# Order of weight splits and new rows, place of the output rows and explicit table loads in a decoder kernel on one core

## Chip, cores and metric

One Trainium2 chip, one of its cores. The metric is the device time of one launch in microseconds: the median over runs. The engines are TensorE (PE in the profile, its weight loads PEld), VectorE (DVE), ScalarE (ACT), GpSimd (POOL) and SyncE (SP), which here only issues DMAs.

## What is computed

The input is x of 256 rows by 1024 columns, fp32. It passes through two blocks of layers, ten residual steps in all:

```python
f = swiglu(rmsnorm(h, g0)) @ w_down;  h = h + 0.5 * rmsnorm(f, g1)     # ffn, four times
h = h + rmsnorm(retention(rmsnorm(h, g2)), g3)                          # layer 0
h = h + rmsnorm(stick_breaking(rmsnorm(h, g2)), g3)                     # layer 1
gate = sigmoid(rmsnorm(h, g6) @ ple_gate); h = h + rmsnorm(gate * (p @ ple_proj), g7)   # twice
h = h + short_conv(rms_norm(h, n0))                                     # second block
h = h + moba(rms_norm(h, n1))                                           # last attention
```

The last attention (moba) has 16 heads of width 64. With 256 rows there is one block of keys, so each head is a causal softmax of q k' with a slope on the distance; q and k are normed per head, and the output rows are multiplied with silu(z) before the last matrix. Everything is fp32 to within small errors, so each matrix product is done as three: high part by high part, high by low, low by high.

## The kernel before

**Weights.** All matrices are streamed once. A slot is 256 rows by 512 columns (512 KB). SP loads it into one of 4 raw buffers (`load_slot`, line 342), each load waiting until DVE has made the low part of the slot four before. ACT rounds it to w_hi (`split`, line 976), DVE makes w_lo = raw - w_hi (`split`, line 1388). w_hi and w_lo are rings of 8 slots; TensorE waits for w_lo (`products`, line 490). `split_to(n)` on either engine means: do all splits up to slot n here. Since the engines run their lists strictly in order, the places of these calls are the schedule, and they are written out by hand.

**Products.** For one slot and one half t of the rows (128 rows) TensorE does six products of 128x128 by 128x512 (lines 497 to 499, two chunks c of three). An "in" phase (`in_proj`, and `ffn` for the four swiglu phases) goes in groups: group m is row half t = m % 2 of 512 output columns, four slots deep (one slot in ple_proj). Groups 2k and 2k + 1 use the same four slots. An "out" phase (`out_proj`) has four groups, two halves by 1024 columns; its last `window` slots (8 for ple_gate, so all of them; 4 where the phase has 8 slots; else 6) are done first for t = 0 and then for t = 1. The order of phases is that of `phase_list` (line 116): ffn_in0, down0, ret_in, ret_out, ffn_in1, down1, ple_proj0, ple_gate0, ffn_in2, down2, sb_in, sb_out, ffn_in3, down3, ple_proj1, ple_gate1, conv_in, conv_out, moba_in, moba_out.

**Boundaries.** After each out phase come new rows h. Boundary b = 0 is the start, 1 down0, 2 ret_out, 3 down1, 4 ple_gate0, 5 down2, 6 sb_out, 7 down3, 8 ple_gate1, 9 conv_out. For each half t and each half q of the columns: TensorE transposes h (`turn_h`, line 531, four transposes), DVE multiplies with the gain into xg (line 1406), ACT rounds to x_hi (line 992), DVE makes x_lo (line 1411). TensorE's group t waits for x_lo of its first half q = 0 before slot 0 and of q = 1 before slot 2 (line 520). Half t = 0 is turned two slots before the end of the out phase. Half t = 1 is turned within group 0 of the next phase: q = 0 after its slot 1, q = 1 after its slot 2 (`turn_new`, line 527), except for boundaries 3 and 7, where `ple` turns it between the groups of ple_proj.

DVE's x_part (line 1401) makes both xg first and then both x_lo:

```python
for q in range(2):
    ... xg[q] = turn[2t + q] * gain          # waits for the transposes
for q in range(2):
    ... x_lo[q] = xg[q] - x_hi[q]            # waits for ACT's x_hi[q]
```

In an out phase DVE and ACT do, in this order: reading of t = 0, splits, x_part(b, 0), reading of t = 1 (ACT: squares of the sums, line 1011, or in ple_gate the sigmoid, line 1165; DVE: gain and residual sum, lines 1422 and 1430), then in the next phase x_part(b, 1). POOL makes the root of the squares between ACT and DVE. In ACT's `start` (line 1038) there are splits up to slot 6 of the phase before x_part(b, 1), then squares of h, then splits up to slot 8. In ACT's `ple` (line 1145) x_part(b, 1) and the squares stand before the fourth copy of sums and the splits of ple_proj's slots 6 and 7, which are slots 4 and 5 of the gate.

**Start.** DVE: gains, x_part(0, 0), splits 0 to 3, then x_part(0, 1). ACT: split 0, x_part(0, 0), split 1, squares, splits up to 5, x_part(0, 1).

**The last attention.** In moba_in groups 8 to 15 TensorE, DVE and ACT run stages 0 to 7 of a pipeline over pairs of heads behind each group (`mb_stage` in three versions). Stage k: TensorE scores of pair k, output of pair k - 2, transposes of the softmax weights of pair k - 1 (`mb_turn_p`, line 855). ACT: copies of the weights of pair k - 1 (line 1330), negated maxima (line 1335) and exponentials (line 1339) of pair k, then two splits. DVE: rows of pair k - 2, distance term and maxima of pair k (lines 1832 to 1837). Groups 12 to 15 are z, which ACT reads with Silu (line 1036). Silu and Exp need different tables; the compiler puts a load before the first activation that needs another table, behind the waits that stand before it.

The first output rows (heads 0 to 3) are turned by `mb_turn_y(0, 0)` (line 895) on TensorE after group 15, ahead of stage 7. ACT makes y_hi of them (line 1344) before it copies the sums of group 15, behind stage 6 and its two splits; DVE makes y_lo (line 1613) behind the same splits. `mb_turn_p(13)`, in stage 7, waits for that y_lo, since it writes the same PSUM bank. Stage 8 runs behind slot 0 of moba_out, stage 9 behind slot 1. In stage 8 `mb_turn_p(15)` waits for y_lo of the next four heads (`mb_turn_y(0, 1)`), which ACT makes behind stage 7; `mb_turn_y(0, 1)` itself waits for ACT's copies of the weights of heads 12 and 13.

Of the kernel before, what the change touches and what calls it, by code (L numbers as in the profile page):

```python
# [36 lines left out]
SC = 2  # L37
# [3 lines left out]
BANKS = 4  # L41
# [171 lines left out]
def build(nc, x, p_in, positions, norm_gains, ffn_w_gate, ffn_w_up, ffn_w_down, ret_w_in, ret_gn_gain,  # L213
          ret_w_out, sb_w_in, sb_w_out, ple_w_gate, ple_w_proj, norm_g_2, conv_w_in_2, conv_w_2,
          conv_w_out_2, attn_w_in_2, q_norm_g_2, k_norm_g_2, attn_w_out_2, consts, out):
    with ExitStack() as ctx:
# [272 lines left out]
        def _(pe):  # L489
            def products(bank, t, n, j, c0, hi, lo, first, last, sign):  # L490

                pe.wait_ge(lo_made, lin(n + 1, RING, j))
                rows = slice(t * P, (t + 1) * P)
                for c in range(SC):
                    a, b = hi[:, c0 + c, rows], lo[:, c0 + c, rows]
                    wh, wl = w_hi[:, n % RING, c, :], w_lo[:, n % RING, c, :]
                    pe.matmul(bank[:, :], a, wh, start=(first and c == 0), stop=False, skip_group_check=True)  # L497
                    pe.matmul(bank[:, :], a, wl, start=False, stop=False, skip_group_check=True)  # L498
                    mm = pe.matmul(bank[:, :], b, wh, start=False, stop=(last and c == SC - 1), skip_group_check=True)  # L499
                if sign is not None:  # L500
                    mm.then_inc(sign, 1)
# [10 lines left out]
            def group(ph, m, hi, lo, j=None, hooks={}, new_x=None):  # L512
# [4 lines left out]
                for s in range(per):  # L517
# [5 lines left out]
                    products(sums[(ph.group0 + m) % BANKS], t, n, j, SC * s, hi, lo, s == 0, last, sign)  # L523
# [3 lines left out]
            def turn_new(b):  # L527

                return {1: lambda: turn_h(b, 1, [0]), 2: lambda: turn_h(b, 1, [1])}
# [356 lines left out]
            def mb_turn_y(half, i):  # L886
# [6 lines left out]
                for c in range(2):  # L893
                    for t in range(NT):
# [7 lines left out]
                     15: lambda: (mb_turn_y(0, 0), mb_stage(7))}  # L902
            hooks.update({8 + k: lambda k=k: mb_stage(k) for k in range(7)})
            in_proj("moba_in", 9, hooks, {10: {2: lambda: mb_turn(1, 1)}})
# [61 lines left out]
        def _(act):  # L966
# [71 lines left out]
            def start(ph, b):  # L1038

                split_to(ph.slot0 + 6)  # L1040
                x_part(b, 1)
                h_squares(b, 1)
                split_to(ph.slot0 + 8)
# [279 lines left out]
            def mb_stage(k):  # L1323

                for hd in range(2 * k - 2, 2 * k) if 1 <= k < MH // 2 + 1 else ():
# [4 lines left out]
                    act.activation(work[:, at + 384:at + 768], mb_p_bank(hd)[:, 0:384], ACT.Copy).then_inc(mb["pt_flat"], 1)  # L1330
                for hd in range(2 * k, 2 * k + 2) if k < MH // 2 else ():
# [15 lines left out]
            for m in range(16):  # L1347
# [11 lines left out]
                if m == 15:  # L1359
                    mb_y_hi(0, 0)  # L1360
# [24 lines left out]
        def _(dve):  # L1385
# [15 lines left out]
            def x_part(b, t):  # L1401
# [7 lines left out]
                for q in range(2):  # L1409
# [134 lines left out]
            x_part(0, 0)  # L1544
# [306 lines left out]
            for k in range(8):  # L1851
                if k == 7:
                    mb_y_lo(0, 0)
                mb_stage(k)
# [37 lines left out]
```

## Time and profile before

| | us |
|---|---|
| median of 3 runs | 1411.66 |
| lowest, highest | 1410.5, 1412.23 |
| the profiled execution | 1412.48 |
| its span in the trace | 1410.7 |
| PE busy | 1389.1 (98%) |
| DVE busy | 845.5 (60%) |
| ACT busy | 728.6 (52%) |
| POOL busy | 66.3 (5%) |
| mean DMA rate | 178 GB/s |

A row of the timeline is: start in us, duration in us, engine, line of the kernel, operation, output <- input, shape, how many are merged, and in brackets the idle time before it and what ended it. The next instruction of ACT or DVE starts about 0.1 us before the end of the one before, so a queue of them is shorter than the sum of durations. Products of 128x512 follow each other every 0.2275 us at full clock though each lasts 0.39: they are pipelined. The granted clock of TensorE is 1.00 at 2.4 GHz and 0.50 at 1.2 GHz.

### The profile page before, as it was taken

Reading aid. Unit: us, or ns where it says so; the run is one execution under the profiler, and the core shown is the slowest. Engines: PE = TensorE matmul, PEld = TensorE weight load, DVE = VectorE, ACT = ScalarE, POOL = GpSimd, SP = SyncE. Lnnn points to the kernel's source line nnn. Section 1 sums busy time; section 2 is a strip of 40 time slices with the busy share of each in tenths; the row PEclk is TensorE's granted clock in tenths of the full one; section 3 lists DMA queues with packets and bytes.
Section 4 is the critical chain, followed back from the end, with each engine's and each line's share of the span. In section 5 each row is a group of like instructions: output and inputs, shape, how many; then the busy total and the mean of one; then the engine's idle time right before and its main releaser. Section 6 shows DMA issues by size and latency. Waiting matters only on the chain. (4 is left out here: it accounts for less than half of the span.)

```text
span 1410.7 us, 19001 instructions
## 1 busy us (share of the span) xinstructions
PE 1389.1 (98%) x6458; PEld 1143.5 (81%) x6458; DVE 845.5 (60%) x1066; ACT 728.6 (52%) x1026; POOL 66.3 (5%) x117
## 2 busy tenths in 40 slices
PE   8999999999999999999999999999999999999998
PEld 6888888888888888878888888878888878888776
DVE  6555766666665555575555554575555675577665
ACT  5444454444454445474444455664444565555683
POOL 1000010000010000010000000010000110002000
PEclk9999999999999999999999999999999999999998
DMA  7656545555645666446567554455666455545431
GB/s 241 190 185 207 183 158 190 180 190 192 201 139 188 194 207 219 153 148 212 178 197 236 164 179 135 135 164 178 188 214 231 143 180 193 182 152 174 147 120 61
DMA packets 186525, 251.41 MB, mean 178 GB/s; under 512 B 15540, under 2 KB 115420, under 8 KB 186460
## 3 DMA queue, kind: packets, MB, share of 16 engines
q1 hardware_dynamic: 186172, 250.43, 55.0%
q8 instruction: 39, 0.64, 0.2%
q14 instruction: 26, 0.21, 0.0%
q10 hardware_dynamic: 288, 0.13, 0.0%
HBM read 249.45 MB, written 1.05 MB: 178 GB/s over the span
## 5 line engine op out<-in xcount | busy, mean ns | idle before, releaser
L1392 DVE TENSOR_TENSOR w_lo<-raw,w_hi 128x1024 fp32r<-128x1024 f32 x460 | 539.6, 1220 | 181.8 <-ACT w_hi L980 180.7
L980 ACT ACTIVATE w_hi<-raw 128x1024 fp32r<-128x1024 f32 x460 | 460.6, 1051 | 135.4 <-PE sums L499 66.9
L497 PE MATMUL sums<-w_hi,x_hi 128*128 128x512 f32 x1312 | 522.4, 398 | 4.8 <-DVE x_lo L1411 3.7
L499 PE MATMUL sums<-w_hi,x_lo 128*128 128x512 f32 x1312 | 512.4, 391 | 0.0
L498 PE MATMUL sums<-w_lo,x_hi 128*128 128x512 f32 x1312 | 511.5, 390 | 0.0
L497 PEld LDWEIGHTS sums<-w_hi,x_hi 128*128 128x128 f32 x1312 | 246.9, 188 | 58.3 <-issue 9.9
L499 PEld LDWEIGHTS sums<-w_hi,x_lo 128*128 128x128 f32 x1312 | 246.5, 188 | 52.1
L498 PEld LDWEIGHTS sums<-w_lo,x_hi 128*128 128x128 f32 x1312 | 247.2, 188 | 49.2 <-issue 1.0
L497 PE MATMUL sums<-w_hi,y_hi 128*128 128x512 f32 x512 | 202.0, 395 | 0.0
L498 PE MATMUL sums<-w_lo,y_hi 128*128 128x512 f32 x512 | 200.0, 391 | 0.0
L499 PE MATMUL sums<-w_hi,y_lo 128*128 128x512 f32 x512 | 200.0, 391 | 0.0
L1053 ACT ACTIVATE work<-sums,stat 128x256 f32<-128x256 f32 x88 | 41.7, 474 | 239.9 <-PE sums L499 239.9
L1468 DVE SCALAR_TENSOR_TENSOR work<-sums,stat,work 128x256 f32<-128x256 f32 x88 | 42.4, 482 | 180.4 <-ACT work L1053 180.4
L499 PEld LDWEIGHTS sums<-w_hi,y_lo 128*128 128x128 f32 x512 | 96.5, 189 | 20.3
L497 PEld LDWEIGHTS sums<-w_hi,y_hi 128*128 128x128 f32 x512 | 96.7, 189 | 19.7
L498 PEld LDWEIGHTS sums<-w_lo,y_hi 128*128 128x128 f32 x512 | 96.6, 189 | 19.5
L1036 ACT ACTIVATE work<-sums,stat 128x512 f32<-128x512 f32 x54 | 37.1, 687 | 129.8 <-PE sums L499 128.6
L992 ACT ACTIVATE x_hi<-xg 128x512 fp32r<-128x512 f32 x40 | 24.8, 630 | 47.3 <-DVE xg L1406 47.0
L924 POOL TENSOR_TENSOR stat<-stat,neg_half 128x1 f32<-128x1 f32 (+1 forms) x48 | 46.3, 964 | 4.0
L938 POOL TENSOR_TENSOR stat<-stat 128x1 f32<-128x1 f32 x16 | 3.6, 223 | 906.6 <-ACT junk L1011 865.1
L1422 DVE TENSOR_TENSOR fg<-sums,post_gain 128x512 f32<-128x512 f32 x24 | 16.6, 692 | 33.3 <-ACT junk L1011 33.1
L1011 ACT ACTIVATE junk<-sums 128x512 bf16<-128x512 f32 x24 | 14.2, 593 | 37.3 <-PE sums L499 37.2
(171 smaller groups left out, 780.9 us busy)
## 6 DMA issues: line engine op xcount, KB each, us to landing
raw<-in_ffn_w_gate_dram SPq DMA_DIRECT2D x176, 256.0 KB, 3.9
raw<-in_ffn_w_up_dram SPq DMA_DIRECT2D x176, 256.0 KB, 4.8
raw<-in_ffn_w_down_dram SPq DMA_DIRECT2D x176, 256.0 KB, 3.9
raw<-in_ret_w_in_dram SPq DMA_DIRECT2D x96, 256.0 KB, 4.0
raw<-in_conv_w_in_dram SPq DMA_DIRECT2D x64, 256.0 KB, 4.0
raw<-in_attn_w_in_dram SPq DMA_DIRECT2D x64, 256.0 KB, 3.9
raw<-in_sb_w_in_dram SPq DMA_DIRECT2D x48, 256.0 KB, 3.6
raw<-in_ret_w_out_dram SPq DMA_DIRECT2D x32, 256.0 KB, 4.5
```

Of the source, the lines that this page charges most:

```text
L497: pe.matmul(bank[:, :], a, wh, start=(first and c == 0), stop=False, skip_group_check=True)
L498: pe.matmul(bank[:, :], a, wl, start=False, stop=False, skip_group_check=True)
L499: mm = pe.matmul(bank[:, :], b, wh, start=False, stop=(last and c == SC - 1), skip_group_check=True)
L924: pool.tensor_tensor(dst, tmp, neg_half[:, 0:k], ALU.pow).then_inc(sign, 1)
L980: act.activation(w_hi[:, n % RING].rearrange("p c n -> p (c n)"), raw[:, n % RAW].rearrange("p c n -> p (c n)"), ACT.Copy).then_inc(hi_mad ...
L992: act.activation(x_hi[:, 4 * q:4 * q + 4, t * P:(t + 1) * P], xg[:, q, :].rearrange("p (c t) -> p c t", c=4), ACT.Copy).then_inc(x_hi_made, 1)
L1011: act.activation(junk[:, 0:COLS], sums[(ph.group0 + 2 * t + n) % BANKS][:, :], ACT.Square, accum_out=f_sq[:, 2 * t + n:2 * t + n + 1]).the ...
L1036: act.activation(dst, sums[(ph.group0 + m) % BANKS][:, :], func, **kw).then_inc(act_read, 1)
L1053: act.activation(work[:, t * FB:(t + 1) * FB], sums[(ph.group0 + m) % BANKS][:, 0:FB], ACT.Silu, scale=r_in[:, t:t + 1]).then_inc(act_read, 1)
L1392: dve.tensor_tensor(w_lo[:, n % RING].rearrange("p c n -> p (c n)"), raw[:, n % RAW].rearrange("p c n -> p (c n)"), w_hi[:, n % RING].rear ...
L1422: dve.tensor_tensor(fg[:, t, n, :], sums[(ph.group0 + 2 * t + n) % BANKS][:, :], post_gain[:, n * COLS:(n + 1) * COLS], ALU.mult).then_inc ...
L1468: dve.scalar_tensor_tensor(out=work[:, HW_HID + t * FB:HW_HID + (t + 1) * FB], in0=sums[(ph.group0 + m) % BANKS][:, FB:2 * FB], scalar=r_i ...
```

## The change

1. Boundaries: DVE's x_part makes xg and x_lo of q = 0 and then xg and x_lo of q = 1. TensorE turns the second half of the rows later: q = 0 in the middle of slot 2 of group 0 instead of after slot 1, q = 1 after slot 2 as before; behind a ple phase (b = 4 and 8) q = 0 after slot 2 and q = 1 in the middle of slot 3. `products` gets a hook after its first chunk for that.
2. Start: DVE makes the low part of slot 0 between xg and x_lo of q = 0. ACT makes splits up to 3, not 5, before x_part(0, 1).
3. Last attention: mb_turn_y(0, 0) stands in the middle of the last slot of group 15; ACT's y_hi of it stands in stage 6 between the copies of weights and the exponentials, DVE's y_lo behind stage 6, ahead of its two splits.
4. ACT loads the table of the exponentials by an explicit instruction in stages 0 and 4 to 7, behind the copies of weights and before the wait for the maxima.

```diff
@@ products (line 490)
-            def products(bank, t, n, j, c0, hi, lo, first, last, sign):
+            def products(bank, t, n, j, c0, hi, lo, first, last, sign, between=None):
...
                     mm = pe.matmul(bank[:, :], b, wh, start=False, stop=(last and c == SC - 1), skip_group_check=True)
+                    if between and c == 0:
+                        between()
@@ group (line 512)
-                    products(sums[(ph.group0 + m) % BANKS], t, n, j, SC * s, hi, lo, s == 0, last, sign)
+                    products(sums[(ph.group0 + m) % BANKS], t, n, j, SC * s, hi, lo, s == 0, last, sign, hooks.get((s, 0)))
                     if s in hooks:
                         hooks[s]()
@@ turn_new (line 527)
-                return {1: lambda: turn_h(b, 1, [0]), 2: lambda: turn_h(b, 1, [1])}
+                if boundaries[b].startswith("ple"):
+                    return {2: lambda: turn_h(b, 1, [0]), (3, 0): lambda: turn_h(b, 1, [1])}
+                return {(2, 0): lambda: turn_h(b, 1, [0]), 2: lambda: turn_h(b, 1, [1])}
@@ TensorE, last attention (line 901)
             hooks = {3: lambda: mb_turn(0, 0), 5: lambda: mb_turn(1, 0), 7: lambda: mb_turn(0, 1),
-                     15: lambda: (mb_turn_y(0, 0), mb_stage(7))}
-            hooks.update({8 + k: lambda k=k: mb_stage(k) for k in range(7)})
-            in_proj("moba_in", 9, hooks, {10: {2: lambda: mb_turn(1, 1)}})
+                     }
+            hooks.update({8 + k: lambda k=k: mb_stage(k) for k in range(8)})
+            in_proj("moba_in", 9, hooks, {10: {2: lambda: mb_turn(1, 1)}, 15: {(3, 0): lambda: mb_turn_y(0, 0)}})
@@ ACT, start (line 1038)
-                split_to(ph.slot0 + 6)
+                split_to(ph.slot0 + (6 if b else 4))
@@ ACT, mb_stage (line 1323)
                     act.activation(work[:, at + 384:at + 768], mb_p_bank(hd)[:, 0:384], ACT.Copy).then_inc(mb["pt_flat"], 1)
+                if k == 6:
+                    mb_y_hi(0, 0)
+                if k in (0, 4, 5, 6, 7):
+                    act.preload_act_table_set("natural_log_exp_and_others")
                 for hd in range(2 * k, 2 * k + 2) if k < MH // 2 else ():
@@ ACT, groups of moba_in (line 1359)
-                if m == 15:
-                    mb_y_hi(0, 0)
@@ DVE, x_part (line 1401)
-            def x_part(b, t):
+            def x_part(b, t, between=None):
...
-                for q in range(2):
+                    if between and q == 0:
+                        between()
                     dve.wait_ge(x_hi_made, 4 * b + 2 * t + q + 1)
@@ DVE, start (line 1544)
-            x_part(0, 0)
+            x_part(0, 0, lambda: split_to(1))
@@ DVE, stages (line 1851)
             for k in range(8):
-                if k == 7:
+                mb_stage(k)
+                if k == 6:
                     mb_y_lo(0, 0)
-                mb_stage(k)
```

## Rows read from the trace of the kernel before

**Rows 1.** The page, costliest groups; and TensorE's waits (us in total, times, longest)

```profile
L1392 DVE TENSOR_TENSOR w_lo<-raw,w_hi 128x1024 fp32r<-128x1024 f32 x460 | 539.6, 1220 | 181.8 <-ACT w_hi L980 180.7
...
PE turn L855 <- DVE y_lo L1613: 3.9, 1, 3.9
PE sums L497 <- DVE x_lo L1411: 3.7, 8, 2.3
```

**Rows 2.** Stretches: us, busy PE, PEld, DVE, ACT, POOL; PEclk, DMA share, GB/s

```profile
20.39:23.48 3.09, 3.09 (x7) 2.45 (x8) 3.09 (x4) 3.07 (x5) 2.29 (x2) 0.50 0.11 15
622.50:624.20 1.70, 0.04 (x1) 0.00 (x0) 0.81 (x2) 1.70 (x4) 1.40 (x4) 1.00 0.22 78
624.20:627.60 3.40, 3.40 (x19) 2.92 (x20) 2.19 (x4) 1.83 (x4) 0.35 (x1) 1.00 0.00 0
...
1378.26:1381.98 3.72, 3.72 (x11) 2.95 (x10) 2.66 (x9) 2.57 (x7) 0.00 (x0) 0.50 0.56 187
```

**Rows 3.** Timeline of the start

```profile
7.31 1.06 ACT L980 ACTIVATE w_hi<-raw 128x1024 fp32r<-128x1024 f32 x1 [4.09 <-DMA raw<-in_ffn_w_up_dram]
...
11.49 0.47 PE L497 MATMUL sums<-w_hi,x_hi 128*128 128x512 f32 x1 [0.76 <-DVE w_lo L1392]
...
20.39 0.76 PE L497 MATMUL sums<-w_hi,x_hi 128*128 128x512 f32 x1 [2.26 <-DVE x_lo L1411]
...
27.41 0.39 PE L497 MATMUL sums<-w_hi,x_hi 128*128 128x512 f32 x1
```

**Rows 4.** Timeline of boundary 1, second half of the rows

```profile
201.42 0.58 ACT L1011 ACTIVATE junk<-sums 128x512 bf16<-128x512 f32 x1
...
205.55 0.33 PE L539 MATMUL turn<-ident,h 128*128 128x128 f32 x1
...
206.24 0.69 DVE L1406 TENSOR_TENSOR xg<-turn,gains_a 128x512 f32<-128x512 f32 x1
...
206.97 0.63 ACT L992 ACTIVATE x_hi<-xg 128x512 fp32r<-128x512 f32 x1 [0.39 <-DVE xg L1406]
...
208.67 1.47 DVE L1411 TENSOR_TENSOR x_lo<-xg,x_hi 128x512 fp32r<-128x512 f32 x2
...
209.61 0.47 PE L497 MATMUL sums<-w_hi,x_hi 128*128 128x512 f32 x1 [0.19 <-DVE x_lo L1411]
```

**Rows 5.** Timeline of boundary 3, ple_proj into the gate

```profile
596.70 1.40 ACT L992 ACTIVATE x_hi<-xg 128x512 fp32r<-128x512 f32 x2 [1.03 <-DVE xg L1406]
...
599.52 3.89 ACT L980 ACTIVATE w_hi<-raw 128x1024 fp32r<-128x1024 f32 x4
600.60 4.63 DVE L1392 TENSOR_TENSOR w_lo<-raw,w_hi 128x1024 fp32r<-128x1024 f32 x4 [1.78 <-ACT w_hi L980]
...
602.01 0.40 PE L497 MATMUL sums<-w_hi,x_hi 128*128 128x512 f32 x1
```

**Rows 6.** Timeline of boundary 4, out of ple_gate0

```profile
619.09 1.25 ACT L1165 ACTIVATE work<-sums,stat 128x512 f32<-128x512 f32 x2
...
624.20 0.33 PE L539 MATMUL turn<-ident,h 128*128 128x128 f32 x1 [1.67 <-DVE h L1430]
...
628.26 0.47 PE L497 MATMUL sums<-w_hi,x_hi 128*128 128x512 f32 x1 [0.19 <-DVE x_lo L1411]
```

**Rows 7.** Timeline of ACT, stage 0 of the last attention

```profile
1317.72 0.20 ACT L1335 ACTIVATE stat<-stat 128x2 f32<-128x2 f32 x1 [4.68 <-DVE stat L1837]
1317.94 1.28 ACT L1339 ACT_TABLE_LOAD   x1
1319.24 0.40 ACT L1339 ACTIVATE work<-work,stat 128x128 f32<-128x128 f32 x1
```

**Rows 8.** Timeline of stages 6 to 8 of the last attention

```profile
1370.51 0.60 PE L895 MATMUL turn<-ident,work 128*128 128x128 f32 x4
...
1377.73 0.87 PE L855 MATMUL turn<-ident,work 128*128 128x128 f32 x3 [3.94 <-DVE y_lo L1613]
...
1384.14 0.69 DVE L1613 TENSOR_TENSOR y_lo<-turn,y_hi 128x512 fp32r<-128x512 f32 x1 [3.06 <-ACT y_hi L1344]
```

## The prediction

> **What bounds the kernel.** I read the waits of TensorE first. It is busy almost throughout, so only its waits can be won, and they are few: 3.9 us before one transpose of the last attention, 3.7 us for low parts of new rows (2.3 of it once, at the start) [rows 1], and 1.7 us for residual rows after each of the two ple phases [rows 6]. Then the granted clock by stretches: it is 0.50 (1.2 GHz instead of 2.4) for some 3 us after the wait at the start and after the wait of the last attention, and stays 1.00 over a 1.7 us wait at 622.5 [rows 2]. Then the timelines around each place that the diff touches [rows 3 to 8]. The reader is to see in them which instruction of ScalarE (ACT) or VectorE (DVE) ends each wait, and how many instructions are queued before it. All waits together, with half clock, are worth under 20 us of 1411; the question is how many are only moved.
>
> **Start.** DVE now makes the low part of slot 0 between the two gain products, and q0's low part before q1's product. Product q0 is long made when w_hi 0, begun at 7.31, ends at 8.37 [rows 3]; w_lo 0 (1.22 [rows 1]) ends 9.6, x_lo q0 (0.69) 10.2, product q1 10.8. TensorE could start at 10.7, when its warming is over, not at 11.49: 0.8 earlier. But ACT does x_hi q1 only at 10.85, so w_hi 1 goes to 11.4 and w_lo 1 ends at 13.7: slot 1 starts at 13.8, after a new 1.8 us wait. Behind it ACT has the squares (1.0) and w_hi 2, so slot 2 waits 0.5 us, to 15.8. Then the transposes, half a slot further in, slots 2 and 3 end at 19.5. ACT has two splits fewer before x_hi of the second half, so its x_lo q0 ends at 19.35 and group 1 starts at 19.6 instead of 20.39 [rows 3], now at full clock. 24 products, one every 0.2275 us at full clock, plus 0.1 put group 2 at 25.1; before it was 27.41 [rows 3]. **-2.3 us.** SP's queue follows the low parts: the load of slot 4 waits for w_lo 0 and goes out a little earlier, those of slots 5 to 7 for w_lo 1 to 3, 1.2 to 1.9 later, and still land before ACT, busy with new rows until 20.4, asks for them; slot 8 waits for w_lo 4, and TensorE comes to it only after 36. ACT's two splits come after the squares, from 21.5 on; w_lo 4 to 7 end at 23.8, 24.9, 26.0 and 27.2 and are read at 25.1, 26.5, 27.8 and 29.2. That slack of 1.3 to 2 us is the cover, so the move costs nothing. The clock after the 1.8 us wait is unknown: bounds 0 (the 1.7 us wait kept 1.00) and +1.5 (half of the 3.09 us at 0.50 [rows 2]). I take 0, the nearer row.
>
> **Ordinary boundaries (b = 1, 2, 5, 6, 9).** Two things happen. For the second half of the rows, x_lo q0 used to queue behind product q1, which waits for the later transpose: product at 206.24, x_hi at 206.97, x_lo only at 208.67, TensorE at 209.61 [rows 4]. Merged, x_lo q0 starts 0.66 after its x_hi (0.63 and the hand-over). From the first transpose to TensorE that is 0.69 + 0.73 + 0.66 + 0.69 + 0.25 (208.67 + 0.69 to 209.61) = 3.03 us. TensorE needed 4.06 us from 205.55 to 209.61, of which 0.36 were waiting; the transpose half a slot (0.7) later leaves it 3.0 us of work: practically no wait. The second transposes stay where they were, and x_lo q1 is ready at 211.2, wanted at 212.1. The w_lo behind it on DVE are 1 us later and wanted only with group 2, 2.7 us after they are made. For the first half the merge costs: product q1, and x_hi q1 on ACT, stand behind x_lo q0, so the squares queued behind x_hi q1, at 201.42 [rows 4], come 1.4 later; the second square is only 0.78 later, since before it waited for its sums. POOL's root, the residual rows and the transpose follow: 205.55 becomes 206.33. Group 1 starts at 206.33 + 3.04 = 209.37 instead of 209.61: -0.24. The same pattern at b = 2 and 5. At b = 6, with a window of four slots, the shift is 0.56: -0.46. At b = 9 no root is in the way: -0.29. **-1.5 us** (bounds: 0, if the delay of the squares takes all; -2.0, if it takes nothing: five waits of 0.36 and a little at b = 6).
>
> **Into ple (b = 3, 7).** The merge acts here too, and TensorE doesn't profit, for it needs x_lo only a slot or more later. ACT's list is: x_hi q0, q1, squares, copy of sums, then w_hi of the fifth gate slot. x_hi starts at 596.70, w_hi at 599.52, w_lo at 600.60 and ends 601.82, and TensorE reads that slot at 602.01 [rows 5]: 0.2 us to spare. Upstream the second square is 0.78 late, which moves x_hi q0 to 597.47; x_hi q1 then waits for x_lo q0 (0.69) and product q1 (0.69): 597.47 + 0.66 + 0.60 + 0.73 = 599.46 instead of 597.47. Everything on ACT behind it is 2.0 later: w_lo ends 603.8, TensorE goes on at 603.96. That is +1.95, twice: **+3.9 us** (between 0, if the cover were larger than I read, and 4.0). This is the term that eats the gains. The next slot's low part is ready 0.2 us before its turn.
>
> **Out of ple (b = 4, 8).** The sigmoids at 619.09 [rows 6] stand on ACT behind x_hi q1, so they and the residual rows are 1.40 later. The transpose of q0 is moved a whole slot (1.37) back, so the wait at 624.20 only moves to 625.6 and stays about 1.85 long. After it, with the second transpose half a slot behind, TensorE has 2.3 us of work and the x_lo chain takes 3.06: group 1 starts at 628.66 instead of 628.26 [rows 6]; the twin gives +0.25. **+0.65 us** (0, if ACT had room for the shift, to +1.4, if nothing of the shift were covered by the later place).
>
> **Last attention, first stage.** ACT's load of the exponential's table stands behind the wait for the maxima; made explicit it lies in an idle stretch of 4.68 us [rows 7]. The first exponentials start 1.28 earlier, and TensorE waited for them at two transposes (1.1 us of idle time, and the transposes' own start and end). **-1.3 us** (bounds: 0 if the load is not taken out of the chain, -1.3 as the whole load). What rows show of the load: 1.28 at 1317.94, and the exponential at 1319.24 [rows 7], so nothing lies between them.
>
> The Trainium skill (ScalarE: Activation LUTs, What ACT_TABLE_LOAD costs) adds a drain of 1380 ns to each load. By that the hidden load would be worth 2.7 us and the sum would be 1.4 us lower; the trace disagrees with it, so the sum does not use it.
>
> **Last attention, end.** The transposes of the output rows, at 1370.51 [rows 8], go in three products earlier, 1369.83; their y_lo on DVE comes before the splits that it stood behind, and is no longer what is late. ACT gains 1.1 per stage in stages 4 and 5 by the explicit loads, and loses it again: in stage 6 it now waits for these transposes. The chain, on the clock of before (without the shift of 1.3): y_hi 1370.46, table 1371.04, maxima 1372.34, exponentials 1372.56 to 1374.58. TensorE transposes the first weights at 1373.5 and the second at 1374.64, not at 1377.73 [rows 8]: 3.1 us won at this place. But ACT sets the next steps as well: two splits to 1376.5, table 1376.6, gate rows 1377.9, weights 1378.5 to 1379.3, table to 1380.6, exponentials 1380.84 to 1382.86, y_hi to 1383.46, y_lo ends 1384.16, where before y_lo began at 1384.14 and ended 1384.83 [rows 8]. TensorE waits 1.6 us for the copied weights, 1.1 for the last score rows on DVE, 1.6 for this y_lo. **-0.8 us**, the rest of the 3.1 is given back. And TensorE stands still for 4.3 of the 6.5 us before it goes on; both rows at 0.50 come after it had stood, 2.3 and 3.9 us, so the clock has likely fallen. Before, the half clock at 1378.26 cost nothing, since y_lo was awaited all the same; now it would fall on products that nothing covers. Bounds 0 (as at 622.5) and +1.9 (half of 3.72 [rows 2]); I take **+1.7**, near the rows at 0.50, because the three waits lie so close together.
>
> **Sum**: -2.3 - 1.5 + 3.9 + 0.65 - 1.3 - 0.8 + 1.7 = +0.35. The profiled execution took 1412.48 (span 1410.7 and 1.8 around it), 0.8 over the median 1411.66. 1412.48 + 0.35 = 1412.8, on the scale of the medians **1412.0**.
>
> **Rivals.**
> - The gate's fifth slot is not late (ACT or DVE finds time I haven't seen): without the 3.9 us, 1408.1; with full clock at the end too, 1406.4. For it: it is the longest chain of small shifts in the sum. Against: 0.2 us of cover is plain [rows 5].
> - The clock stays at 1.00 in the last attention: 1410.3. For it: no single wait there is above 1.7 us.
> - **Slower**: each new wait of 1.8 to 1.95 us (one at the start, two at the gates) also halves the clock. The point that decides lies between the 1.67 us of idle time before 624.20, after which the clock stayed at 1.00, and the 2.26 before 20.39 [rows 2, 3, 6]; the new waits would count as 1.6 to 1.8, near the lower end. Price 1.5 each, 4.5 in all: 1416.5; with two of them 1415.0.
> - The change doesn't do what it says: the explicit loads are added to the compiler's, not put in their place. Then the 1.3 us are not won, and stages 6 and 7 have one more load each in the chain, 2.6 us: 1415.9.
>
> **How the numbers follow.** Forecast 0.42, gate not late 0.22, clock full 0.15, more half clock 0.15, added loads 0.03, something else 0.03. About 0.2% (2.8 us) is what a measurement tells from no change. Only the first rival goes below 1408.9: faster 0.25. The halvings and added loads go above 1414.5: slower 0.20. Same 0.55. The range takes in the first rival with full clock and the slower one with two halvings: 1406.4 to 1415.0.
>
> **What would show it.** Right: no wait for x_lo at the start of group 1 of the ordinary boundaries; a wait of about 1.95 us for w_lo in the middle of both gate phases; group 2 of the first phase at 25.1; a transpose of weights in the last attention near y_lo's end, and half clock after it. Wrong: no wait for w_lo at the gates, or a clock below 1.00 there. In the last attention, the sum of waits before the first output product falls from 3.9 to about 1.2, and two new ones follow it.

## The result and the profile after

Slower. Over 13 runs the changed kernel took 1415.05 us in the median (1413.53 to 1418.50), the kernel before, measured beside it, 1411.66 (1410.43 to 1412.52): a ratio of 1.0027 with an interval of 1.0019 to 1.0035, slower by 0.27%. The forecast was 1412.0 with a range up to 1415.0, and "within 0.2%" as the likeliest case. The measured median is 0.05 above the top of that range.

| us | before | after |
|---|---|---|
| median | 1411.66 | 1415.05 |
| the profiled execution | 1412.48 | 1415.68 |
| its span | 1410.7 | 1413.9 |
| PE busy | 1389.1 (98%) | 1389.4 (98%) |
| DVE busy | 845.5 | 846.3 |
| ACT busy | 728.6 | 729.7 |

The engines do the same work; 3.2 us of span are new waiting or slower clock. The waits of TensorE after the change (answer to [rows 1]; us in total, times, longest):

```profile
PE sums L497 <- DVE w_lo L1398: 5.6, 4, 1.8
PE turn L543 <- DVE h L1437: 4.2, 5, 1.7
...
PE turn L859 <- DVE y_lo L1620: 1.5, 1, 1.5
PE turn L899 <- ACT work L1334: 1.5, 1, 1.5
PE turn L859 <- ACT work L1347: 1.2, 3, 0.6
PE sums L497 <- DVE x_lo L1418: 1.1, 2, 0.6
PE turn L872 <- DVE work L1839: 0.8, 1, 0.8
```

The 3.9 us before one transpose are gone, and the 3.7 for x_lo are down to 1.1 (at the ordinary boundaries they are gone, as forecast). In their place stand waits for w_lo (one at the start and one in each gate, as I call the two ple_gate phases, about 1.75 each), and four waits at the end of the last attention instead of one. The waits for the residual rows h after the ple phases are as long as before; those at boundaries 1, 2 and 5 have grown from 0.12 to 0.27 each.

**Start** (answers to [rows 3]). Slot 1 waits 1.73 us, slot 2 0.37, group 2 begins at 24.61 instead of 27.41. The clock is 1.00 throughout.

```profile
9.97 0.47 PE L497 MATMUL sums<-w_hi,x_hi 128*128 128x512 f32 x1
13.32 0.47 PE L497 MATMUL sums<-w_hi,x_hi 128*128 128x512 f32 x1 [1.73 <-DVE w_lo L1398]
15.31 0.47 PE L497 MATMUL sums<-w_hi,x_hi 128*128 128x512 f32 x1 [0.37 <-DVE w_lo L1398]
19.06 0.48 PE L497 MATMUL sums<-w_hi,x_hi 128*128 128x512 f32 x1
24.61 0.39 PE L497 MATMUL sums<-w_hi,x_hi 128*128 128x512 f32 x1
```

**Gate of the first ple phase** (answers to [rows 5]). The two x_hi, which shared one row before, now start 1.99 us apart, since the second product stands behind the first x_lo. ACT reaches w_hi of the fifth slot late, and TensorE waits 1.77 us.

```profile
594.35 0.63 ACT L996 ACTIVATE x_hi<-xg 128x512 fp32r<-128x512 f32 x1 [1.03 <-DVE xg L1412]
596.34 0.63 ACT L996 ACTIVATE x_hi<-xg 128x512 fp32r<-128x512 f32 x1 [1.36 <-DVE xg L1412]
598.39 3.89 ACT L984 ACTIVATE w_hi<-raw 128x1024 fp32r<-128x1024 f32 x4
599.47 4.63 DVE L1398 TENSOR_TENSOR w_lo<-raw,w_hi 128x1024 fp32r<-128x1024 f32 x4 [1.77 <-ACT w_hi L984]
600.75 0.50 PE L497 MATMUL sums<-w_hi,x_hi 128*128 128x512 f32 x1 [1.77 <-DVE w_lo L1398]
```

What follows is in the stretches (columns as in [rows 2]): behind each gate's wait come 3.4 us at 0.50. In the last attention, where the forecast had the half clock, it is 1.00.

```profile
598.33:600.75 2.42, 0.65 (x4) 0.19 (x2) 1.28 (x2) 2.42 (x4) 0.55 (x1) 1.00 0.00 0
601.75:605.15 3.40, 3.40 (x9) 2.63 (x8) 2.35 (x3) 1.81 (x2) 0.00 (x0) 0.50 0.84 254
...
1127.40:1130.80 3.40, 3.40 (x10) 2.66 (x9) 2.94 (x3) 2.40 (x3) 0.00 (x0) 0.50 0.70 238
1381.00:1388.00 7.00, 3.39 (x23) 2.44 (x21) 4.77 (x15) 6.59 (x17) 0.00 (x0) 1.00 0.47 150
```

**Last attention, stage 0** (answers to [rows 7]). ACT loads the table at 1316.95, in idle time, but the maxima come late: DVE waits for the root until 1318.09, makes two w_lo, and ACT's first step behind the maxima starts at 1322.80. At this place the changed kernel runs 3.9 us behind the kernel before, so this is 1.2 later than the 1317.72 of [rows 7]. The first exponential, at 1323.04, comes only 0.1 earlier than before on the shifted clock: what the load saved is gone.

```profile
1316.95 1.28 ACT L1338 ACT_TABLE_LOAD   x1
1318.09 1.29 DVE L1800 TENSOR_TENSOR work<-work,stat 128x512 f32<-128x512 f32 x2 [3.31 <-POOL stat L928]
1319.30 2.35 DVE L1398 TENSOR_TENSOR w_lo<-raw,w_hi 128x1024 fp32r<-128x1024 f32 x2
1322.80 0.20 ACT L1343 ACTIVATE stat<-stat 128x2 f32<-128x2 f32 x1 [4.57 <-DVE stat L1844]
```

**Last attention, end** (answers to [rows 8]). ACT stands idle 3.71 us before y_hi, and the load and the exponentials of stage 6 are queued behind it. TensorE then meets four waits.

```profile
1374.30 0.60 ACT L1352 ACTIVATE y_hi<-turn 128x512 fp32r<-128x512 f32 x1 [3.71 <-PE turn L899]
1374.91 1.28 ACT L1338 ACT_TABLE_LOAD   x1
...
1378.59 0.55 PE L859 MATMUL turn<-ident,work 128*128 128x128 f32 x3 [0.56 <-ACT work L1347]
...
1383.34 0.63 PE L899 MATMUL turn<-ident,work 128*128 128x128 f32 x4 [1.47 <-ACT work L1334]
1384.79 0.43 PE L872 MATMUL turn<-post_gain,work 128*128 128x64 f32 x2 [0.82 <-DVE work L1839]
...
1388.19 0.52 PE L859 MATMUL turn<-ident,work 128*128 128x128 f32 x3 [1.52 <-DVE y_lo L1620]
```

### The profile page after: what moved, and what is told of

It reads as the page before. It is cut to its first block and busy times, and to the rows that moved or that the text cites. A ratio compares the mean times of both kernels' runs of the same rounds, so it can differ in the third digit from the quotient of the medians.

```text
span 1413.9 us, 19001 instructions
## 1 busy us (share of the span) xinstructions
PE 1389.4 (98%) x6458; PEld 1142.4 (81%) x6458; DVE 846.3 (60%) x1066; ACT 729.7 (52%) x1026; POOL 63.0 (4%) x117
## 5 line engine op out<-in xcount | busy, mean ns | idle before, releaser
L1418 DVE TENSOR_TENSOR x_lo<-xg,x_hi 128x512 fp32r<-128x512 f32 x40 | 27.7, 693 | 27.2 <-ACT x_hi L996 27.2
```

The costliest lines, as they stand in the source:

```text
L1418: dve.tensor_tensor(x_lo[:, 4 * q:4 * q + 4, t * P:(t + 1) * P], xg[:, q, :].rearrange("p (c t) -> p c t", c=4), x_hi[:, 4 * q:4 * q + 4, ...
```

## The experiments

In each trace I compare the start of the same weight product with that in the trace of before. A step in this difference is the price of what lies between two such products ("by the marks", below). The step is read at the first product behind a wait; behind a gate's wait it grows by another 0.1 over the next product. The diffs are condensed to the lines that matter. Medians of "before" beside the runs lay between 1410.97 and 1412.22, so medians of different experiments are good to about a microsecond, the steps to some 0.05. At the start the traces differ by more: in the trace of before the first weight tile landed later than in all others (the first w_hi begins at 7.31 there, at 6.79 in the changed kernel's and at 6.48 to 7.05 in the rest).

### Gates: undo the order, shorten the wait, move the splits

**no_merge_ple**, in DVE's x_part of the changed kernel:

```diff
+if b in (3, 7): product(0); product(1); low(0); low(1)
+else:           product(0); low(0); product(1); low(1)
```

> The changed kernel with the old order of products and low parts at the two boundaries into ple (b = 3, 7) alone. Theory A (the loss is the gate's fifth slot: two waits of 1.77 us for its low part, each followed by 3.4 us at half clock, 3.69 + 3.65 = 7.3 us): both waits and both stretches at 0.50 go, about 1407.7 us. Rival B (the stretches at 0.50 come whatever the wait is, since they moved there from the end of the last attention): the waits go, 3.5 us, the half clock stays, 1411.5. Rival C (what is won at the gates is lost again out of ple): 1415.

Measured: 1410.02 (11 runs; ratio to before 0.9988, 0.9979 to 0.9997). Both waits and both stretches at 0.50 are gone, 7.3 us by the marks, but now the last attention's end shows 0.50 from 1377.3 to 1384.1, at 1.5 us. So A holds for the waits. Its 1407.7 was 2.3 too low, since it did not ask where else the clock would fall.

**gate_short**: the old order for `b in (3, 7) and t == 0` alone.

> The changed kernel with the old order for the first half of the rows alone at b = 3 and 7. The chain to the fifth slot's low part then loses the late squares (0.78) but not the wait of the second high part for the first low part: the wait should be about 1.1 us instead of 1.77. Theory A on the clock (a short wait leaves it at 1.00): 3.69 + 3.65 becomes 1.1 + 1.1, about 1410. Rival (any late slot at this place halves it for 3.4 us): 1.1 + 1.7 each, about 1413.4.

Measured: 1412.47 (11 runs). The step at the fifth slot is 1.10 and 1.09 (waits of 0.94 and 0.93 us), with no half clock behind it: A's mechanism. The 1410 was missed because the end has its half clock in this trace, at 1.6 by the marks. In ten of the runs the time is 1411.95 to 1413.28 and in one 1410.64, so nothing in the times asks for a halved gate beside the end's, but only one execution was traced.

**splits_first**, in both engines' `ple`: `split_to(ph.slot0 + 6)` becomes `+ 8`.

> The changed kernel, merged order kept everywhere, but in both ple phases ScalarE and VectorE split the two slots behind the sixth before the new rows of the second half, not after them. The fifth slot of the gate is then long ready. Theory A (the cost is the place of these splits in the queue behind the new rows): no wait in the middle of the gates, no half clock there; the new rows come 2 to 2.5 us later instead, which the first half's eight slots cover (11 us): about 1407.8. Rival (the new rows are then late for the gate's second half, or the residual rows out of ple by the same 2 us): 1410 to 1412.

Measured: 1420.41 (5 runs), 5 us worse than the changed kernel: both theories wrong. The tile of the eighth slot had not landed, and behind this DMA wait ACT kept the copies that free ple_proj's banks and all new rows:

```profile
594.82 1.06 ACT L984 ACTIVATE w_hi<-raw 128x1024 fp32r<-128x1024 f32 x1 [2.07 <-DMA raw<-in_ple_w_gate_dram]
```

```profile
596.41 0.80 PE L497 MATMUL sums<-w_hi,x_hi 128*128 128x512 f32 x1 [2.97 <-ACT work L1040]
```

The first is ACT, the second TensorE's first gate product, 3.2 us late. The clock was at 0.50 from 596.1 to 599.5, which cost another 1.5. The fifth slot itself had no wait any more.

**split7**: the same with `+ 7`.

> The changed kernel, merged order kept; before the new rows of the second half both engines split one slot more in the ple phases (seven, not six), so that the fifth slot of the gate is ready before them. Its tile was already loaded in the trace with two slots more; only the eighth came late, 594.82. Theory A (the place in the queues is the cause of the wait, not the work itself): no wait at the fifth slot, 0.3 to 0.5 us at the sixth, no half clock: 6 us less than with both gates halved, 1411. Rival (the new rows are then late by as much and TensorE waits for them instead): 1413.

Measured: 1413.62 (10 runs). The fifth slot has no wait; the sixth waits instead (1.58 and 1.59 by the marks, not 0.3 to 0.5). I had forgotten that ACT's next w_hi is now behind the new rows in the fifth's place. Of the gates' cost mainly the half clock is gone: there was no halving behind these waits of 1.45 and 1.44 us. The end has its half clock in this trace, at 1.3.

### The end: loads, and the place of the output rows

**loads_only**, the kernel before with, in ACT's mb_stage:

```diff
+if k in (0, 4, 5, 6, 7):
+    act.preload_act_table_set("natural_log_exp_and_others")
```

> The kernel before with the explicit table loads of the last attention alone. Theory A (the load at stage 0 is worth what the forecast said, and only the merged order at b = 9 took it back by making the maxima late): the tenth group starts 1.2 to 1.3 us earlier than in the kernel before, and about as much is gained at the end of the run; 1410.4. Rival (maxima are not later for the order at b = 9, the gain is small by itself): under 0.3 us at that place.

Measured: 1405.67 (4 runs; ratio 0.9956, 0.9940 to 0.9971), 5.7 us faster than before. Stage 0 gives 1.28, as A says. The end gives 4.4, which neither theory expected: the first output product comes 3.49 us earlier, the first twelve run at full clock where most of them had 0.50 before (1.71 more), and 0.76 is taken back at the next wait. ACT's queue shows why:

```profile
1364.29 0.86 ACT L1330 ACTIVATE work<-turn 128x384 f32<-128x384 f32 x2
1365.17 1.28 ACT L1332 ACT_TABLE_LOAD   x1
1366.46 0.20 ACT L1337 ACTIVATE stat<-stat 128x2 f32<-128x2 f32 x1
...
1370.60 0.57 ACT L1346 ACTIVATE y_hi<-turn 128x512 fp32r<-128x512 f32 x1
```

Load and exponentials of stage 6 run while TensorE is still at the last group, and y_hi comes after them with nothing to wait for.

**rows_old**, the changed kernel with the old place of the output rows:

```diff
-                if k == 6: mb_y_hi(0, 0)          # ACT, ahead of stage 6's load
+                if m == 15: mb_y_hi(0, 0)         # ACT, behind its splits
-                if k == 6: mb_y_lo(0, 0)          # DVE
+                if k == 7: mb_y_lo(0, 0)
-            15: {(3, 0): lambda: mb_turn_y(0, 0)} # PE
+            15: lambda: (mb_turn_y(0, 0), mb_stage(7))
```

> The changed kernel with the output rows of the last attention back in their old place (transposed after the last group, high part on ScalarE behind stage 6's splits, low part ahead of stage 7 on VectorE); everything else as changed, the explicit loads too. Theory A (the new place makes stage 6's load and exponentials on ScalarE wait for the transposes, and that costs what the explicit loads win): the end is that of the kernel with the loads alone, which was 4.4 us shorter than before from the sixteenth group on; here 3.8 us less than the changed kernel, no half clock at the end, so 1410.5 to 1412 by how often the gates are halved. Rival B (the new place was a gain of its own, and the loads bring the rest only with it): 1415 to 1418. Rival C (no part in it): 1415.3.

Measured: 1408.84 (11 runs; ratio 0.9987, 0.9978 to 0.9996), 6.2 below the changed kernel. From the sixteenth group to the end it is 4.43 us shorter than before; the changed kernel's 0.61. Two products show it, the first of the sixteenth group's last slot and the thirteenth of the output phase, in before, in the changed kernel and here:

```profile
1369.15 0.39 PE L497 MATMUL sums<-w_hi,x_hi 128*128 128x512 f32 x1
1385.25 0.47 PE L497 MATMUL sums<-w_hi,y_hi 128*128 128x512 f32 x1
...
1372.98 0.39 PE L497 MATMUL sums<-w_hi,x_hi 128*128 128x512 f32 x1
1388.47 0.47 PE L497 MATMUL sums<-w_hi,y_hi 128*128 128x512 f32 x1
...
1369.91 0.39 PE L497 MATMUL sums<-w_hi,x_hi 128*128 128x512 f32 x1
1381.58 0.47 PE L497 MATMUL sums<-w_hi,y_hi 128*128 128x512 f32 x1
```

They lie 16.10, 15.49 and 11.67 us apart. So the new place costs 3.8 by waits alone. The rest of the 6.2 would be half clock, of which this trace has none as long as weight products run. Seven of the times lie at 1408.3 to 1409.3 and four at 1410.3 to 1410.4, which fits one stretch more in those four, but none of them was traced. A's mechanism is right. Its time, 1410.5 to 1412, was too high, because it expected halved gates more often than they came.

**both_undone**: rows_old and no_merge_ple together.

> The changed kernel with two of its parts undone together: the old order at the two boundaries into ple, and the old place of the output rows. Theory A (these two are the loss, they lie 790 us apart and add up: 4.1 us at the gates without half clock, 3.8 at the end): rows_old's 1408.8 less 4.1 = 1404.7, fast runs near 1404.4 by its marks, and all other parts of the change together are a gain of some 7 us. Rival (undoing one brings the half clock, or the wait, back at the other): 1406.5.

Measured: 1404.46 (5 runs within 0.4; ratio 0.9949, 0.9935 to 0.9962). Undoing the two parts takes 10.6 us off the changed kernel's time, which is the sum of the two single results (5.0 and 6.2) to within the noise. All its other parts together are a gain of 7 to 8.

### Stage 0

**no_load0**: without the load at k = 0.

> The changed kernel without the explicit table load of the last attention's first stage. Theory A (the load does leave the chain, and what it saved was taken back because the maxima come 1.2 us later): the compiler's own load, 1.28 us, stands behind the maxima again, and the time rises by 1.2 to 1.3 us to about 1416.3. Rival (the load was worth nothing here, TensorE waits for something else): no change, 1415.1.

Measured: the step at the tenth group is +1.18 instead of -0.09. The load did leave the chain. The median, 1417.82 of 4 runs, is 2.8 up, not 1.3. The mean clock of the four runs, 0.998 in the traced one and 0.995 to 0.996 in the other three, says that more of them had several stretches at 0.50 (next part).

**no_merge_9**: the old order for `b == 9` alone.

> The changed kernel with the old order at b = 9 alone. Theory A (the 1.2 us that the maxima of stage 0 are late come from the merged order at b = 9, whose gaps VectorE never fills again before stage 0): the 0.36 us won at the start of the last attention's second group are lost, stage 0 gives 1.2 us instead of 0.09: net 0.8 faster than the changed kernel. Rival (the order at b = 9 has nothing to do with it): 0.36 us slower, stage 0 as before.

Measured: stage 0 -1.22, the second group +0.01 instead of -0.36, as A says; 1415.39 (8 runs), where the net of 0.8 drowns in the clock. This profile has 0.50 at both gates and at the end.

### The clock, and the two halves of the boundary change

**after_again**: no edit.

> The changed kernel once more, unedited. Theory A (the same waits halve the clock in some executions and not in others: the run without the load at stage 0 waited as long at both gates, 1.93 us, and kept 1.00 there, and had the stretch at 0.50 at the end instead): the times lie in groups 1.7 us or more apart, near 1413.9 (one stretch, at the end), 1415.6 (one gate more, or the gates without the end) and 1418 (all three), and this profile may show other places than the first. Rival B (the places are fixed by the program): both gates at 0.50 and 1.00 at the end again.

Measured: 1415.67 (7 runs: six at 1415.1 to 1416.5, one at 1418.83, and none near 1413.9 where A expected a group). The waits at the gates and at the end are the same to 0.02 us, the clock is not. It is 1.00 behind both gates and 0.50 at the end, so B is wrong:

```profile
600.80:604.20 3.40, 3.40 (x15) 2.80 (x16) 3.24 (x3) 2.70 (x3) 0.00 (x0) 1.00 0.68 186
1125.40:1128.80 3.40, 3.40 (x15) 2.77 (x16) 3.20 (x3) 2.67 (x3) 0.00 (x0) 1.00 0.68 224
...
1384.00:1390.70 6.70, 5.86 (x16) 4.73 (x17) 4.22 (x10) 4.62 (x6) 0.00 (x0) 0.50 0.00 0
```

**merge_only**: the kernel before with the merged order at all boundaries.

> The kernel before with the merged order of products and low parts at every boundary alone (transposes, start and last attention as before). Theory A: gates +1.94 each, with or without 1.7 us of half clock each; ordinary boundaries as in the changed kernel or a little later (the residual rows are as late and their transposes stand half a slot earlier, so TensorE waits for them there): -0.2 each; out of ple +0.4 and +0.2; stage 0 1.2 us later, end as before: 1415.5, to 1419 with both gates halved. Rival (the merged order is a gain outside ple by itself, and the loss at the gates the only one): 1414.

Measured: 1423.98 (4 runs), 13 us slower than before: both theories wrong. The gates' waits come as A says (+1.93 each), the second with half clock behind it. At boundaries 1, 2 and 5 the step is +0.47 instead of -0.2, at 6 it is +0.25, and only 9, which has no root in the way, gains 0.36: the late residual rows are now awaited at the old place (0.94 us at 205.92), which costs more than the gain for x_lo. Out of ple +2.6 and +2.3, because the wait before the transpose grows to 3.02 and the clock falls:

```profile
627.91 1.09 PE L539 MATMUL turn<-ident,h 128*128 128x128 f32 x4 [3.02 <-DVE h L1431]
```

```profile
628.00:631.40 3.40, 3.40 (x11) 2.71 (x12) 1.90 (x3) 1.57 (x2) 0.27 (x1) 0.50 0.00 0
```

**places_only**: the kernel before with the later transposes alone.

> The kernel before with the later places of the residual rows' transposes alone (half a slot, a whole one after ple), old order everywhere. The merged order with the old places was 12 us slower than the changed kernel's neighbour in this respect: it waited 2.6 and 2.3 us more out of ple. Theory A (places and order only pay together: the low part of the first quarter still stands behind the second product): ordinary boundaries 0 to +0.1 us; out of ple the second transpose comes 0.7 us after the first, not 1.4, so -0.5 to -0.7 each: 1410.3. Rival (the places are the gain, the order is none): -0.2 at each ordinary boundary and -1 or more out of ple: 1408.5.

Measured: 1407.90 (10 runs; ratio 0.9974, 0.9965 to 0.9983). Boundaries 1, 2, 5 and 6 give 0.30 to 0.34 each, 9 gives nothing, out of ple come -0.7 and -0.85. At the ordinary boundaries the rival is right, out of ple the values lie between the two theories. That is 2.8 us; another 1.9 of this trace are at the start, where it has the clock at 1.00 (about 1.5) and the first tile 0.5 earlier than the trace of before. At b = 1 the transpose, which before came 0.51 us after the last product's start (0.23 is the pace), now comes without a wait, and x_lo follows the two transposes, now 1.14 us apart, not 1.87. The later places are a gain of their own. The merged order takes from it at boundaries 1, 2 and 5 (-0.20 in the changed kernel) and adds to it at 6 and 9 (-0.43 and -0.36).

### A version that beats both

**best1** adds to these findings: old order for the first half and into ple, merged for the second half elsewhere, and

```diff
+mb_norm(1, 1, lambda: split_to(s0 + 22))     # DVE: two w_lo within the wait for the root
+if k == 7: mb_y_hi(0, 1)                     # ACT: behind the load, ahead of the exponentials
+if m == 14: mb_y_hi(0, 0)                    # ACT: behind stage 6's exponentials
```

> A combination. From the changed kernel it keeps the start, the merged order for the second half of the rows outside ple, the later first transposes of residual rows (now after the ple phases too, half a slot, not a whole one) and all explicit loads. The old order is back for the first half of the rows everywhere and at both boundaries into ple. New: at stage 0 the two low parts of weights go into VectorE's wait for the root (3.31 us); at the end y_hi of the first output rows stands behind stage 6's exponentials, and that of the second ahead of stage 7's. By the marks of the changed kernel without half clock (1412.2): gates 2 x 1.95, out of ple 2 x 1.2, ordinary boundaries 0.6, stage 0 about 0.5, end 3.7 less: about 1401. Rival (ScalarE at the end only trades one late transpose for another, as the change did): 1404 to 1405, with half clock at the end 1406.

Measured: 1399.28 (5 runs; ratio 0.9914, 0.9901 to 0.9928). The boundaries b = 1, 2, 5 and 6 give 0.68 each, b = 9 0.36, out of ple 1.02 and 1.19, stage 0 1.41, the end 4.7, and the clock stays at 1.00 from the start to the last product. It is 1.7 us better than the forecast of 1401: against the changed kernel the ordinary boundaries gave 1.7, not 0.6, and stage 0 gave 1.3, not 0.5.

**best2** is best1 with another start:

```diff
-            x_part(0, 0); split_to(2); h_squares(0, 0)                # ACT
+            x_part(0, 0, lambda: split_to(2)); split_to(4); h_squares(0, 0)
-            x_part(0, 0, lambda: split_to(1))                         # DVE, one call
+            x_part(0, 0, lambda: split_to(split_next[0] + 1))         # called twice
```

> The combination, with another start: ScalarE makes w_hi of slot 1 between the two high parts of the first rows, in an idle time of 2.0 us, and w_hi 2 and 3 ahead of the squares; VectorE makes w_lo of slot 1 between the second product and its low part. Slot 1 then starts with no wait or little (1.8 less), slots 2 and 3 and group 1 1.5 to 2.5 us earlier: about 1397.3. Rival (the tile of slot 1 has not landed by 8.5 us, or the second half's new rows set group 1 anyway): under 1 us, 1398.7.

Measured: 1397.52 (4 runs; ratio 0.9906, 0.9891 to 0.9921), 13.5 us below before. Group 1 starts at 17.40, not 19.13. TensorE's waits that are left:

```profile
PE turn L541 <- DVE h L1454: 1.9, 2, 1.0
PE turn L857 <- ACT work L1347: 0.8, 2, 0.6
...
PE sums L497 <- DVE w_lo L1399: 0.3, 1, 0.3
```

## Why the prediction was wrong

Its terms against the two traces of the changed kernel (trace 1 is that of the result, trace 2 that of after_again; both against the profiled 1412.48):

| term | forecast | trace 1 | trace 2 |
|---|---|---|---|
| start | -2.3 | -2.80 | -2.92 |
| ordinary boundaries, five | -1.5 | -1.34 | -1.36 |
| waits at the gates | +3.9 | +4.1 | +4.1 |
| half clock at the gates | 0 | +3.2 | 0 |
| out of ple | +0.65 | +0.57 | +0.57 |
| stage 0 | -1.3 | -0.09 | -0.10 |
| end, waits | -0.8 | -0.6 | -0.6 |
| half clock at the end | +1.7 | 0 | +2.7 |
| rest | 0 | +0.2 | +0.2 |
| sum | +0.35 | +3.2 | +2.6 |

(In trace 1 the gates' steps are 3.69 and 3.65 together with the clock; 4.1 of it is what trace 2 shows at full clock, a step of 1.94 at the first product and 0.1 behind it, twice. At the end the step is 2.14 in trace 2, which less the -0.6 of trace 1 makes 2.7.)

**Right.** The start, the ordinary boundaries, the way out of ple and the gates' wait came out within 0.2 us each (the start within 0.6: the first product began at 9.97, not 10.7, for the first w_hi began 0.5 earlier in this execution). The start's 2.8 is not all the edit's: places_only, without that edit, shows 1.9 there, so the edit itself may be worth only about 0.9; no run undid it alone. The end's waits came where they were forecast and nearly as long (1.5, 0.8 and 1.5 against 1.6, 1.1 and 1.6), and that the 3.1 us are "given back" is so.

**The step that failed most** is the clock at the gates. The forecast put the new waits of 1.8 to 1.95 us nearer to the 1.67 at which the clock had stayed and took 0; a halving was only a rival. In trace 1 both gates were halved, for 3.2 us in all, and the forecast had itself named a clock below 1.00 there as a sign of being wrong. In trace 2 neither was. The runs show that neither 0 nor 1.5 is the number: after the same wait (1.94 by the marks) five of the twelve gates in the traces with it had 0.50 behind them (both in trace 1 and in no_merge_9, one in merge_only) and seven had not (both in trace 2, no_load0 and rows_old, one in merge_only). Since merge_only has both outcomes in one execution, it is not the chip either. The times fall into groups: six of the first 13 runs lie at 1413.5 to 1414.4, five at 1415.05 to 1415.7, two at 1418.4 and 1418.5. The gaps of 1.5 and 3.1 between them are about one and two halved gates, at 1.6 each by the marks, but of these 13 executions one was traced. In the same traces the 1.7 us wait out of ple never lowered the clock, and the shorter gate wait of gate_short did not either. What decides behind a wait of 1.77 us stays open. The Trainium skill (TensorE: Matmul & The Clock Gate, What's actually happening) says that the hardware watches TensorE's activity on a time base that runs freely and does not begin with the kernel. The two traces of one program agree with it, but do not prove it. A forecast should have carried the halving as a share: five of twelve at 1.6 to 1.7 each, which for two gates is +1.4 in all.

**The second step** is stage 0, and it failed in both traces. The load was worth its 1.28 (loads_only, no_load0); the sum took it in full and did not ask what else comes later there. The merged order at b = 9, which the forecast costed at -0.29 without its downstream, makes the maxima 1.2 us late: no_merge_9 gives it back (in merge_only, with the transposes at their old place, the same order makes them 0.6 late). DVE makes up none of this delay between these boundary rows and stage 0. The Trainium skill (ScalarE: Activation LUTs, What ACT_TABLE_LOAD costs) counts a drain with each load, 2.66 us in all; the measured step of 1.28 disagrees.

**The scale.** The forecast took the start's -2.3 from a trace that has a stretch at 0.50 there, and then took 0.8 off once more to go from this trace to the median of before. That counts part of the same clock twice. Among the runs of before that were measured beside the experiments, all but one of those below 1411.5 have a mean clock of 0.997 and all above have 0.996, so the median lies between executions with and without one stretch more. That it is the one at the start is likely, as only one execution was traced. Without the 0.8 the forecast would have been 1412.8.

**The half clock at the end**, forecast at 1.7, was right as a mean and in neither of the two traces. Of the eight traces with the output rows in the new place, seven have it, at 1.3 to 2.7 us (2.7 in trace 2), and trace 1 has none. The mean of the eight is 1.6. In trace 1 its absence hides half of what the halved gates cost; that the sum is off by no more there is luck.

With both steps right, +0.35 becomes +0.35 + 1.2 + 1.4 = +2.95, against 3.4 between the medians. The agreement is partly chance, since the start's 0.5 and the 0.8 of the scale are left out and work against each other.

The blind spot beside them did not make an error in the sum, but in the reading. The -0.8 of the end was taken as one thing. It is two: the loads, which are worth 4.4 there (loads_only, rows_old), and the place of the output rows, which costs 3.8. I did not test which of the four loads it is. The same holds for the boundaries: later transposes, a gain, and merged order, a loss into ple and, at most boundaries, for the first half of the rows.

## What to carry to other kernels

Cost each edit alone before you cost them together: a net loss of 3.4 us was a gain of 7 and a loss of 11 here, and the good parts kept alone are worth more than the whole. On an engine that runs its list in order, an instruction that waits for another engine belongs behind the work that needs nothing, not ahead of it: the output rows turned early, with y_hi before the exponentials, cost 3.8 us, the split ahead of a tile that had not landed 5. Where a change gives TensorE a new wait like the 1.77 us at the gates here, behind which the clock was halved five times in twelve, run the same program several times and look for groups in the times; one trace shows one of them.

## What the runs showed of the hardware beyond that

- One program, waits equal to 0.02 us: 0.50 behind both gates in one execution, and behind none, but at the end, in another. In merge_only both happened in one execution, 1.00 behind the first gate's wait of 1.77 us and 0.50 behind the second's.
- The longer wait is not always the one that halves the clock. Before group 1 of the first phase TensorE waited 2.26 us in before and 2.21 in loads_only, and the clock was 0.50 after it. It waited 2.33 in places_only and 2.42 in merge_only, and the clock stayed at 1.00. The forecast's reading, that the deciding length lies between 1.67 and 2.26, does not hold. Two of the four, loads_only and merge_only:

```profile
20.00 0.47 PE L497 MATMUL sums<-w_hi,x_hi 128*128 128x512 f32 x1 [2.21 <-DVE x_lo L1413]
20.80:24.20 3.40, 3.40 (x10) 2.63 (x9) 3.40 (x4) 3.37 (x4) 2.15 (x2) 0.50 0.38 116
...
21.41 0.47 PE L497 MATMUL sums<-w_hi,x_hi 128*128 128x512 f32 x1 [2.42 <-DVE x_lo L1412]
21.41:24.80 3.39, 3.39 (x15) 2.82 (x16) 2.69 (x4) 3.01 (x5) 1.17 (x2) 1.00 0.00 1
```

- Explicit table loads replace the compiler's own: before, the changed kernel and loads_only have 17 loads each. Where ACT was idle, at stage 0 in loads_only, the whole 1.28 us went.
- A stretch at 0.50 after a gate lasted 3.4 us in each trace; at the end of the last attention it lasted 6.8 us in six of seven (1383.9 to 1390.8 in trace 2) and 3.4 in one (split7).
- With no wait of TensorE above 1.4 us once its products run (best1), five runs lay at 1398.2 to 1401.3; with best2, four within 0.9 us.
